# Row maxima of three attentions: products over 128 rows instead of 64, from the second block of queries on

## What is computed

```
# dense_attn, called for each block of 128 queries
s = einsum("bqkgd,bskd->bkgqs", q, k)         # 1024 + 256 keys
p = softmax(s, axis=-1)
o = einsum("bkgqs,bskd->bqkgd", p, v)

# fox_attention: keys up to the query, a bias c[q] - c[k], a causal mask
sc = einsum('bqhd,bkhd->bhqk', qb, kb) * scale
sc = where(mask, sc + bias, NEG_BIG)
pr = softmax(sc, axis=-1)
```

## Time and profile before

| | us |
|---|---|
| median of 3 runs | 3843.76 (3840.67 to 3855.43) |
| the profiled execution's own time | 3830.29 |
| its span | 3828.5 |
| PE busy in the span | 3604.5 (94%) |
| first layer's attention, from its second block's maxima on | 446 to 705 |
| second layer's | 1336 to 1572 |
| forgetting attention | 2606 to 2775 |

### The profile page before, as it was taken

One profiled execution on the slowest core, in us unless ns is written; L12 is line 12 of the kernel. 1 busy time (PEld: TensorE's weight loads), 2 busy tenths in 40 slices (PEclk: granted clock), 3 DMA queues, 4 the chain that ended last, 5 costly groups with the idle time before them and its releaser, 6 DMA issues. The chain is left out here.

```text
span 3828.5 us, 54923 instructions
## 1 busy us (share of the span) xinstructions
PE 3604.5 (94%) x22742; PEld 2749.3 (72%) x22742; DVE 2058.1 (54%) x2358; ACT 1207.3 (32%) x1716; POOL 1875.7 (49%) x1064
## 2 busy tenths in 40 slices
PE   5999899889899999899999998989999899999998
PEld 5888544578788744578887777876577788878877
DVE  4443577553444466563466734545542788874242
ACT  3234344431223344432123422324401444441020
POOL 1443266544255266544355643303633699973433
PEclk9999899999999999999999999998999899999999
DMA  5112200025211200022221230020043122224112
GB/s 185 39 39 68 70 1 1 26 90 201 74 39 62 54 1 1 26 100 89 83 72 50 75 95 24 4 100 1 1 137 115 63 82 93 83 104 167 60 50 72
DMA packets 101935, 258.02 MB, mean 67 GB/s; under 512 B 29232, under 2 KB 38576, under 8 KB 100800
## 3 DMA queue, kind: packets, MB, share of 16 engines
q1 hardware_dynamic: 83008, 215.42, 16.5%
q10 hardware_dynamic: 18688, 39.20, 3.1%
HBM read 200.02 MB, written 54.56 MB: 66 GB/s over the span
## 5 line engine op out<-in xcount | busy, mean ns | idle before, releaser
L1846 PE MATMUL acc<-h_hi,weights_hi 128*128 128x512 f32 (+1 forms) x928 | 347.3, 374 | 7.7 <-DVE h_lo L2015 5.3
L1091 DVE TENSOR_REDUCE part_max<-aux 128x1 f32<-128x428 f32 (+5 forms) x468 | 252.8, 581 | 179.7 <-PE aux L932 128.2
L1847 PE MATMUL acc<-h_lo,weights_hi 128*128 128x512 f32 (+1 forms) x928 | 338.6, 365 | 0.0
L1848 PE MATMUL acc<-h_hi,weights_lo 128*128 128x512 f32 (+1 forms) x928 | 338.4, 365 | 0.0
L2553 PE MATMUL acc<-h_hi,weights_hi 128*128 128x512 f32 x672 | 271.9, 405 | 0.0
L2555 PE MATMUL acc<-h_hi,weights_lo 128*128 128x512 f32 x672 | 263.2, 392 | 0.0
L2554 PE MATMUL acc<-h_lo,weights_hi 128*128 128x512 f32 x672 | 262.9, 391 | 0.0
L2029 DVE RECIPROCAL arena<-arena 128x512 f32<-128x512 f32 (+1 forms) x48 | 141.7, 2953 | 223.3 <-ACT arena L1992 223.3
L1053 ACT ACTIVATE probs<-acc 128x1024 f32<-128x1024 f32 (+1 forms) x168 | 168.4, 1003 | 252.6 <-PE acc L967 252.0
L978 PE MATMUL acc<-probs,v_tok 128*64 128x512 f32 (+3 forms) x864 | 222.4, 595 | 2.2 <-DVE inverse L1111 2.2
L3721 PE MATMUL acc<-operand_hi,weights_hi 128*128 128x512 f32 x504 | 197.3, 391 | 10.8 <-POOL weights_lo L3455 10.8
(11 more groups left out here) (525 smaller groups left out, 9167.4 us busy)
## 6 DMA issues: line engine op xcount, KB each, us to landing
weights<-in_w_in SPq DMA_DIRECT2D x44, 512.0 KB, 3.5
arena<-in_w_mod SPq DMA_DIRECT2D x6, 2048.0 KB, 8.8
weights<-in_w_up SPq DMA_DIRECT2D x24, 512.0 KB, 4.2
weights<-in_w_out SPq DMA_DIRECT2D x22, 512.0 KB, 4.9
weight_sums<-feed_forward_spill SPq DMA_DIRECT2D x22, 512.0 KB, 4.6
xT<-in_w_up SPq DMA_DIRECT2D x20, 512.0 KB, 4.2
weights<-in_w_mod SPq DMA_DIRECT2D x4, 2048.0 KB, 26.5
mixer_gates<-arena SPq DMA_DIRECT2D x32, 256.0 KB, 2.0
```

What stands on the lines that cost most here:

```text
L1091: nc.vector.tensor_reduce(part_max[:, b % 2, j, hh, i:i + 1], max_tile(m)[:, hh, 0:cw], AX_X, ALU.max, negate=True).then_inc(max_done, 1)
L1846: nc.tensor.matmul(out, w_hi[:, b, k, :], hi[:, k, cols], start=(k == 0), stop=False)
L1847: nc.tensor.matmul(out, w_hi[:, b, k, :], lo[:, k, cols], start=False, stop=False)
L1848: return nc.tensor.matmul(out, w_lo[:, b, k, :], hi[:, k, cols], start=False, stop=(k == KD - 1))
```

## The change

From the second block of queries on (b >= 1), the product of line 932 takes all 128 rows of qs and of k_twice, in place of the 64 of `halves[hh]`; columns, queries and destination stay. The first block's pieces (b = 0) stay as they are. At the first piece of each block with b >= 1, PE waits in addition for q_parted of the pair.

```diff
                         if b >= 1:
+                            pe.wait_ge(q_parted, 2 * p + 2)
                             pe.wait_ge(row_copied, b)
                     for hh in range(2):
+                        rows = slice(0, P) if b else halves[hh]
                         if b >= 1:
                             pe.wait_ge(max_done, 2 * m - 1 + hh)
                         elif m >= 2:
                             pe.wait_ge(max_done, 2 * m - 3 + hh)
-                        mm = nc.tensor.matmul(max_tile(m)[:, hh, 0:cw], qs[halves[hh], p % 2, hh, qb:qb + P],
-                                              keys(p, hh)[0][halves[hh], c0:c0 + cw], start=True, stop=not further)
+                        mm = nc.tensor.matmul(max_tile(m)[:, hh, 0:cw], qs[rows, p % 2, hh, qb:qb + P],
+                                              keys(p, hh)[0][rows, c0:c0 + cw], start=True, stop=not further)
```

## The result

The changed kernel takes 3814.04 us (median of 6, 3812.19 to 3834.33) against 3842.22 us for the kernel before (median of 6 beside it). The medians are 28 us apart; the ratio, which is the measure from here on, is 0.9934, with a 95% interval of 0.991 to 0.9959: 25 us less, give or take 10. The profiled execution of the changed kernel took 3815.39 us, its span is 3813.6.

The account below looks back on a forecast made before the run. PE's instruction order was taken to bound all three attentions. Gains of 10.7 + 7.9 = 18.6 us, less 1.5 for the wait and some 2 for VectorE or ScalarE, gave -15: 3829 us in the median's terms, range 3808 to 3850.

Parts of the forecast that it names:

- the likeliest case: Whole kernel: shorter steps around the maxima pieces with the clock unchanged, giving 3829 us, range 3819 to 3838, chance 0.57.
- signs of being wrong: 0.39 staying behind 128-row products, waits for part_max growing by the gain, or half-clock stretches changing by more than 10 us.
- Steps between shapes: Around 128-row maxima on PE: 0.23 in after scores, 0.28 out to values, line 967 after 0.72 instead of 0.98.
- Rival (b): At every maxima piece: 0.39 and 0.33 are start-up, so only the heads' overlap is lost; +27, 3871 us, chance 0.06.
- (d): At all 220 changed pieces: each 128-row product leaves its weight load uncovered; +48, 3892 us, chance 0.02.
- the pieces that values follow, taken as 0: 102 pieces between scores and values in the two layers: 0.72 now, 0.70 changed, counted as no gain.
- the wait of 0.25 is covered: 30 pieces between values and scores: the second head's wait for VectorE vanishes as the former piece started 0.10 sooner; gain 0.25 each.
- the forgetting attention's 7.9 us: Its 44 pieces, both shape changes gone: 23 gain 0.16 and 21 gain 0.2 each, 3.7 + 4.2 us.
- The wait, forecast at 1.5: PE's new wait for q_parted: +1.5 us at the first layer's last pair, 0 at the other eight pair changes.
- The clock, taken as 0: Half clock in some 34 us of the three attentions: more rows might save at most 17 us, counted as 0.
- Rival (a): In the attentions' half-clock stretches the clock comes up sooner: -24 us in all, 3820, chance 0.20.
- Rival (c): In each block VectorE's chain sets the time and PE waits longer: within 5 us, 3841, chance 0.15.

## Why the prediction was right, and where it was not

The direction, the time (3829 against 3814, inside the range of 3808 to 3850) and the mechanism of the steps were right. The measured time is outside the 3819 to 3838 that the likeliest case had for itself, and below 3824.6, where the prediction put a chance of 0.37. The sum was not right: its terms were off in both directions. And one of the prediction's own signs of being wrong came true: the half-clock stretches inside the attentions changed by 34 us, where it named 10. The two other signs did not: the values follow a 128-row piece by 0.28, and the waits of line 932's weight loads for VectorE in the second layer went from 40.4 to 35.6 us.

**Steps between shapes.** Each came out as worked: 0.23 into the piece, 0.28 out to the values, 0.73 instead of 0.98 where scores follow. Rival (b), a start-up of every piece, and (d), an open weight load in each, are both refuted by these rows: the piece between scores and values has stayed at 0.71.

**Mis-sized: the pieces that values follow, taken as 0.** In the second layer, summed over the starts, the pieces that scores follow went down by 7.8 us (6.7 in the groups at full clock) and those that values follow went up by 3.0. In the groups of the first layer that ran at full clock in both kernels it is 4.2 down and 2.8 up, which leaves little there. The step that failed is "the wait of 0.25 is covered": true for that piece, but VectorE's two reductions then end later against PE's order, and the next piece's second head waits for them. The experiment with 128 rows only before scores shows that this is not the overlap: with 64 rows there the layer is as long.

**Mis-sized: the forgetting attention's 7.9 us.** At full clock 2642 to 2769 against 2630 to 2753 shows 4 us for three and a half pairs, some 5 in all. One reason stands in the rows of the changed kernel, against the earlier trace rows:

```profile
2644.19 0.23 PE L971 MATMUL acc<-causal,ident_rounded 128*128 128x128 f32 x1
2644.25 0.69 PE L934 MATMUL aux<-k_twice,q_both_parts 128*128 128x512 f32 x2
2644.78 0.63 PE L940 MATMUL aux<-c_parts,minus_row 128*128 128x512 f32 x2
2645.33 0.65 PE L980 MATMUL acc<-probs,v_tok 128*64 128x256 f32 x4
```

0.06 into the piece as forecast, but 0.53 for its two heads and not 0.46: the mask's 128 columns stream for 0.06 and cannot hide a weight load of 0.11. From the mask's product to the values it is 1.14, where it was 1.24 (2661.56 to 2662.80): 0.10 gained and not 0.16. The steps of all three attentions gave some 11 to 12 us where 18.6 was forecast, or 16.6 with the 2 that it took off for VectorE.

**The wait, forecast at 1.5.** Alone it costs 4.0 us in the first layer, by the stand of 2 us and the clock that follows it. In the changed kernel 0 and 3.4 us at half clock follow the stand, in its two profiles, and I put the cost at some 1 us. The place was right, and so was the price in the changed kernel; with 64 rows it was low.

**The clock, taken as 0.** This was the largest miss: some 14 us, against 17 as the bound. Rival (a) was right in kind, with 0.20. The forecast said that the trace did not show what 64 rows count for, which was true of one profile. Why the whole-array products raise it stays open: rows fed, columns streamed and the stops between shapes all changed together. More columns alone did not do it at the two starts (0.60 and 0.64), 65 rows in one head did it in the forgetting attention and not in the first layer, and whole-array work between 64-row pieces did it at the starts and not behind them. The forecast came near in part by luck: 5 us too much in the steps, and 14 too little in the clock, partly cancel. In the profiles the forecast of -15 was met (3815.39 against 3815), but only because the unchanged rest of the span was 10 us longer than in the profile of before, 8 of them for 17 us more at half clock.

**Rival (c),** absorption, holds for some 3 us in each layer and no further.

## What to carry to other kernels

In this kernel a small product in another row shape costs a stop of 0.10 us and an open weight load of 0.11 at each change of shape. Where its operands have the full height, the same columns over the whole array cost no more, though two halves ran side by side before (0.71 against 0.72). Where PE is the bound and its clock dips, count half-clock stretches as part of an edit's effect, and compare them over several profiles: inside the attentions most came again at the same place, while outside them they moved the span by up to 30 us between two executions of one kernel. And follow each saved step to the next wait of the same buffer.

## What was not expected of the hardware

- The half-clock stretches at the start of an attention are reproducible: 10.2 and 6.8 us at the start of the forgetting attention in all four profiles in which all its maxima are over 64 rows and no work is added, none in the changed kernel's two. Single stretches of 3.4 us elsewhere come and go.
- The doubled product over 64 rows left the granted clock at 0.60 and 0.64 at the starts of the first layer and of the forgetting attention, while one head over 128 rows and the other over 65 had 0.76 and 1.00, and both over 128 rows 1.00 and 1.00.
- Making one 64-row product twice costs 0.20 us where it is exposed (0.59 against 0.39): these two products in the same rows did not overlap.
- A stand of PE of 2.06 us cost 4.0 us where 10.2 us at half clock followed it, and by the estimate above some 1 us where none did.
